# Last norm's row sums moved to TensorE, one tile's scale to GpSimd, spare input loads dropped, last row stores split over two queues, one chunk's weight sums moved

## The reference, cut to what matters

```python
x = layer_norm(ALPHA * x + h, ln1_g, ln1_b)        # ALPHA: 2**0.25, then 4**0.25
# every token goes to its two best of 16, 32 and 32 experts, with weights w1 and w2
f = w1 * expert_a(x) + w2 * expert_b(x)            # expert: (silu(x @ gate) * (x @ up)) @ down
x = layer_norm(ALPHA * x + f, ln2_g, ln2_b)
def layer_norm(u, g, b):
    mu = mean(u); var = mean((u - mu)**2)
    return (u - mu) * rsqrt(var + 1e-5) * g + b
```

## Time and profile before

| | us |
|---|---|
| three runs | 2676.49, 2680.26, 2680.79 (median 2680.26) |
| the profiled execution's own time | 2675.48 |
| its span, first to last instruction | 2673.8 |
| PE busy | 2275.1 (85%) |
| DVE busy | 1024.7 (38%) |
| ACT busy | 561.3 (21%) |
| POOL busy | 290.2 (11%) |
| mean granted TensorE clock, as a share of 2.4 GHz | 0.951 |

### The profile page before, as it was taken

One profiled execution on the slowest core, in us unless ns is written; L12 is line 12 of the kernel. 1 busy time (PEld: TensorE's weight loads), 2 busy tenths in 40 slices (PEclk: granted clock), 3 DMA queues, 4 the chain that ended last, 5 costly groups with the idle time before them and its releaser, 6 DMA issues. The chain is left out here.

```text
span 2673.8 us, 86507 instructions
## 1 busy us (share of the span) xinstructions
PE 2275.1 (85%) x37544; PEld 1611.2 (60%) x37545; DVE 1024.7 (38%) x2635; ACT 561.3 (21%) x1213; POOL 290.2 (11%) x493
## 2 busy tenths in 40 slices
PE   8997988788799888999667789978888988779972
PEld 3445546666588745777545543458887466656751
DVE  1206342222553844333212263046765352223324
ACT  2036211111301721111001131034442111111111
POOL 1001222222100010000000010012333100000001
PEclk9998999999899999999988899989999999999996
DMA  8602169998404008889999942000001289999995
GB/s 341 258 32 95 49 248 368 408 375 321 165 32 160 1 18 323 347 327 428 429 428 428 395 144 102 0 25 3 3 5 65 81 343 427 429 428 428 404 428 218
DMA packets 92529, 635.86 MB, mean 238 GB/s; under 512 B 22869, under 2 KB 43609, under 8 KB 58346
## 3 DMA queue, kind: packets, MB, share of 16 engines
q1 hardware_dynamic: 47984, 584.42, 53.0%
q0 software_dynamic: 13008, 29.41, 3.5%
q10 hardware_dynamic: 31402, 20.06, 2.4%
HBM read 588.69 MB, written 45.12 MB: 237 GB/s over the span
## 5 line engine op out<-in xcount | busy, mean ns | idle before, releaser
L1315 PE MATMUL ps<-ring,arena 128*32 128x128 f32 x13184 | 413.2, 285 | 107.8 <-DMA ring<-in_experts 73.5
L1315 PEld LDWEIGHTS ps<-ring,arena 128*32 128x32 f32 x13184 | 382.2, 115 | 152.7 <-DMA ring<-in_experts 71.9
L1379 ACT ACTIVATE arena<-ps 128x64 f32<-128x64 f32 x292 | 65.5, 224 | 1075.9 <-PE ps L1315 962.0
L1531 DVE TENSOR_TENSOR arena<-arena,ps 128x64 f32<-128x64 f32 x292 | 64.7, 222 | 590.6 <-ACT arena L1379 590.6
L1326 PE MATMUL ps<-ring,arena 128*32 128x256 f32 x3296 | 205.0, 384 | 34.6 <-DVE arena L1534 20.6
L1292 PE MATMUL ps<-x_tok,arena 128*32 128x256 f32 x3456 | 214.9, 388 | 15.8 <-DVE arena L1434 8.2
L1315 PE MATMUL ps<-arena 128*32 128x128 f32 x5504 | 175.1, 287 | 51.3 <-DMA arena<-in_experts 40.0
L1315 PEld LDWEIGHTS ps<-arena 128*32 128x32 f32 x5504 | 161.5, 115 | 70.9 <-DMA arena<-in_experts 45.5
L1265 PE MATMUL ps<-ring,arena 128*128 128x512 f32 x384 | 171.9, 604 | 3.4 <-PEq L2696 1.7
L1326 PEld LDWEIGHTS ps<-ring,arena 128*32 128x32 f32 x3296 | 106.7, 110 | 111.6 <-issue 29.0
L1292 PEld LDWEIGHTS ps<-x_tok,arena 128*32 128x32 f32 x3456 | 119.1, 113 | 74.0 <-issue 24.7
(11 more groups left out here) (476 smaller groups left out, 3106.8 us busy)
## 6 DMA issues: line engine op xcount, KB each, us to landing
ring<-in_experts SPq DMA_DIRECT2D x165, 2048.0 KB, 21.7
arena<-in_experts SPq DMA_DIRECT2D x50, 2048.0 KB, 24.4
xt_mem<-in_experts SPq DMA_DIRECT2D x25, 2048.0 KB
ring<-in_mixer_chunks SPq DMA_DIRECT2D x24, 2048.0 KB, 13.3
xybuf<-arena ACTq DMA_DIRECT2D x608, 32.0 KB, 6.8
xybuf<-arena SPq DMA_DIRECT2D x1, 9216.0 KB, 51.5
xbuf<-arena SPq DMA_DIRECT2D x1, 9216.0 KB, 31.7
arena<-xbuf POOLq DMA_DIRECT2D x176, 32.0 KB, 6.4
```

Of the source, the lines that this page charges most:

```text
L1315: ins = pe.matmul(ps[at, 2 + half, 0:P], xg[:, k, :], w_gu[half][:, k, q, :], start=(k == 0), stop=(k == NK - 1))
L1379: act.activation(silu_g[:, half, :], ps[:, 2 + half, 0:HALF], ACT.Silu).then_inc(s_silu[half], 1)
L1531: dve.tensor_tensor(hidden[:, half, :], silu_g[:, half, :], ps[:, 2 + half, HALF:P], ALU.mult)\
```

## The change

Four edits.

1. `store_quarters` takes the engine. Behind the loop ACT stores quarters 0 and 1 of the last block, SP quarters 2 and 3, in all three layers. SP does so behind all its weight loads.
2. Layer 0: POOL's loop of input loads runs one turn less (8 DMAs of 32 KB less), and its last wait is for 64 counts less of each buffer.
3. `norm_qkv_stage`: `weight_sums(1)` stands behind `update_rows(3)`.
4. `last_norm_stage` is written anew. DVE makes nine diagonal matrices (alpha, and w1 and w2 of each tile on the diagonal) from the identity. PE sums alpha x + w1 y1 + w2 y2 in PSUM with them, six products of 128x512 for each tile, those with alpha of tiles 0 and 1 ahead of the gathers. DVE takes the statistics, ACT normalizes, both from PSUM. POOL does `gain_rows` of tile 0, DVE of tiles 1 to 3, each behind the statistics of the next tile. The second gather of tile 0 has a semaphore of its own.

```diff
--- before.py
+++ after.py
@@ -1148,6 +1148,11 @@
+            def store_quarters(eng, start, b, two):
+                for q in two:
+                    eng.dma_start(xybuf[bass.ds(start, BLK), q * W:(q + 1) * W], y_sb[quarters[q], b, :])\
+                       .then_inc(s_stored[b], 16)
+
             def value(eng, n, low=1, high=MAXB):
...
@@ -1184,6 +1189,9 @@
                             load_chunk(sp, n)
+                    fours = value(sp, slice(E + 2, E + 3), high=MAXB // AHEAD)
+                    sp.wait_ge(s_y, AHEAD * fours + 1)
+                    store_quarters(sp, AHEAD * fours * BLK, AHEAD - 1, (2, 3))
...
@@ -1215,16 +1223,16 @@
                         pool.wait_ge(*at_step("placed", TABLED))
-                        fours = value(pool, slice(E + 2, E + 3), high=MAXB // AHEAD)
+                        fours = value(pool, slice(E + 2, E + 3), 2 * T // BLK // AHEAD, MAXB // AHEAD)
                         pool.wait_ge(*at_step("inputs_sent", 2 * NT * 16))
                         load_inputs(3 * BLK, 0)
-                        with pool.Fori(0, fours) as p:
+                        with pool.Fori(0, fours - 1) as p:
                             for b in range(AHEAD):
...
                         for b in range(AHEAD):
-                            pool.wait_ge(s_loaded[b], fours * 64 + 64)
+                            pool.wait_ge(s_loaded[b], fours * 64)
...
@@ -1357,14 +1365,9 @@
-                    def store_quarters(start, b, two):
-                        for q in two:
-                            act.dma_start(xybuf[bass.ds(start, BLK), q * W:(q + 1) * W], y_sb[quarters[q], b, :])\
-                               .then_inc(s_stored[b], 16)
-
                     act.wait_ge(*at_step("places_ready", 2))
                     for b in range(AHEAD - 1):
-                        store_quarters((SPARE_BLOCK + b) * BLK, b, range(4))
+                        store_quarters(act, (SPARE_BLOCK + b) * BLK, b, range(4))
                     act.wait_ge(*at_step("placed", TABLED))
...
@@ -1374,11 +1377,11 @@
                             for half in range(2):
-                                store_quarters(g * BLK, freed, (2 * half, 2 * half + 1))
+                                store_quarters(act, g * BLK, freed, (2 * half, 2 * half + 1))
                                 act.wait_ge(s_gu[half], g + 1)
...
                     act.wait_ge(s_y, AHEAD * fours + 1)
-                    store_quarters(AHEAD * fours * BLK, AHEAD - 1, range(4))
+                    store_quarters(act, AHEAD * fours * BLK, AHEAD - 1, (0, 1))
                     for b in range(AHEAD):
...
@@ -1555,39 +1558,94 @@
+        second_rows_in = signal("second_rows_of_tile_0_gathered")
+
         def last_norm_stage(alpha, w1, w2, slots_i):
             y1, y2 = view(arena, NK * T, NT, D), view(arena, 2 * NK * T, NT, D)
-            n0, l0, d0, o0 = tail_bases(), loaded.total, dve_b.take(NT), stored.take(16 * NT)
+            diag0, sum0, scaled0 = dve_a.take(2), mm.take(NT), pool_chain.total
+            alpha_diag, *w_diag = (view(slot(0), n * P, P) for n in range(2 * NT + 1))
+            n0, l0, d0, o0 = tail_bases(), loaded.total, dve_b.take(NT - 1), stored.take(16 * NT)
             with nc.Block() as block:
...
                     for j in range(NT):
-                        sp.wait_ge(dve_b.sem, d0 + j + 1)
+                        if j == 0:
+                            sp.wait_ge(pool_chain.sem, scaled0 + 2)
+                        else:
+                            sp.wait_ge(dve_b.sem, d0 + j)
                         sp.dma_start(out[0, j * P:(j + 1) * P, :], x_tok[:, j, :]).then_inc(stored.sem, 16)
...
                 def _(pool):
-                    gather_rows(pool, y1, y2, slots_i)
+                    for j in range(NT):
+                        for n, (y, there) in enumerate(((y1, rows_in[j]), (y2, rows_in[j] if j else second_rows_in))):
+                            pool.indirect_dma_start(out=y[:, j, :], out_offset=None, in_=xybuf,
+                                                    in_offset=bass.IndirectOffsetOnAxis(ap=slots_i[:, n, j:j + 1], axis=0))\
+                                .then_inc(there.sem, 16)
+                    pool.wait_ge(loaded.sem, l0)
+                    pool.wait_ge(ln_done.sem, n0["normed"] + 1)
+                    gain_rows(pool, Chain(pool, pool_chain), 0).then_inc(pool_chain.sem, 1)
+
+                @block.tensor
+                def _(pe):
+                    def add(diag, rows_of, j, **group):
+                        for c in range(2):
+                            ins = pe.matmul(ps[:, 2 * j + c, :], diag, rows_of[:, j, c * CH:(c + 1) * CH], **group)
+                        return ins
+
+                    pe.wait_ge(dve_a.sem, diag0 + 1)
+                    for j in range(2):
+                        add(alpha_diag, x_tok, j, start=True, stop=False)
+                    pe.wait_ge(dve_a.sem, diag0 + 2)
+                    for j in range(NT):
+                        if j >= 2:
+                            add(alpha_diag, x_tok, j, start=True, stop=False)
+                        pe.wait_ge(rows_in[j].sem, n0["rows"][j] + (32 if j else 16))
+                        add(w_diag[j], y1, j, start=False, stop=False)
+                        if j == 0:
+                            pe.wait_ge(second_rows_in.sem, 16)
+                        add(w_diag[NT + j], y2, j, start=False, stop=True).then_inc(mm.sem, 1)
...
                 def _(act):
-                    alpha_rows(act, alpha)
+                    act.preload_act_table(ACT.Sqrt)
                     for j in range(NT):
-                        norm_rows(act, j, n0)
+                        mv = mean_var[:, j, :]
+                        act.wait_ge(stat.sem, n0["stat"] + j + 1)
+                        act.activation(mv[:, 2:3], mv[:, 1:2], ACT.Sqrt, bias=eps_ln).then_inc(sq.sem, 1)
+                        act.wait_ge(scaled.sem, n0["scales"] + j + 1)
+                        act.activation(x_tok[:, j, :], ps[:, 2 * j:2 * j + 2, :].rearrange("p c n -> p (c n)"), ACT.Identity,
+                                       bias=mv[:, 1:2], scale=mv[:, 3:4]).then_inc(ln_done.sem, 1)
...
+                    def statistics(j):
+                        mv = mean_var[:, j, :]
+                        dve.wait_ge(mm.sem, sum0 + j + 1)
+                        for c in range(2):
+                            ins = dve.bn_stats(sums[:, j % 2, 6 * c:6 * c + 6], ps[:, 2 * j + c, :])
+                        link(ins)
+                        dve.bn_aggr(mv[:, 0:2], sums[:, j % 2, :]).then_inc(stat.sem, 1)
+                        dve.wait_ge(sq.sem, n0["sq"] + j + 1)
+                        link(dve.reciprocal(mv[:, 3:4], mv[:, 2:3]))
+                        dve.tensor_scalar(mv[:, 1:2], mv[:, 0:1], mv[:, 3:4], -1.0, ALU.mult, ALU.mult).then_inc(scaled.sem, 1)
+
                     def finish(j):
...
+                    dve.tensor_scalar(alpha_diag, ident, alpha, None, ALU.mult).then_inc(dve_a.sem, 1)
+                    for j in range(NT):
+                        for n, wn in enumerate((w1, w2)):
+                            ins = dve.tensor_scalar(w_diag[n * NT + j], ident, wn[:, j:j + 1], None, ALU.mult)
+                    ins.then_inc(dve_a.sem, 1)
                     dve.wait_ge(loaded.sem, l0)
                     for j in range(NT):
-                        update_rows(dve, link, j, n0, y1, y2, w1, w2)
-                        if j > 0:
+                        statistics(j)
+                        if j > 1:
                             finish(j - 1)
...
@@ -1835,9 +1893,8 @@
                     for j in range(NT):
-                        if j == 3:
-                            weight_sums(1)
                         update_rows(dve, link, j, n0, y1, y2, w1, w2)
+                    weight_sums(1)
                     dve.wait_ge(act_b.sem, n0["taken"] + 2 * NT)
...
```

## The result

The changed kernel takes 2666.49 us (median of 6 runs, 2654.63 to 2671.29) against 2680.18 (6 runs, 2676.49 to 2680.99). The ratio is 0.9947, 95% interval 0.9926 to 0.9968: 13.7 us less, where 14.6 were forecast; the interval is 8.6 to 19.8 us, so that the two lie so close is in part luck. The profiled execution took 2666.24 (span 2664.5, before 2673.8), so it shows only 9.3 of it. Single executions of the changed kernel lie up to 17 apart, and in the ten profiled executions of this document layer 0's last copy of rows, which only the spare loads precede of what the edits touch, starts anywhere from 675.83 to 682.07. So I compare stretches, each from one event of the program to another, and not whole times.

The account below looks back on a forecast made before the run. It took POOL's drain to bound layer 0's end, waits for tile 3 the norm behind, and DVE the last norm. Terms 4.65 + 0 + 0.95 + 4.2 + 4.8 = 14.6 gave 2665.7 us against 2680.3, range 2659 to 2673.

Parts of the forecast that it names:

- Layer 0's end: Barrier behind layer 0: without spare loads POOL's drain ends earlier and split stores bound the stage; 4.65 us won.
- the rival of a 13 us drain: Layer 0's end: POOL's drain lasts 13 as in layers 1 and 2, so only 1.6 us won; chance 0.10.
- Layer 1's end: Split stores behind SP's weight chunks: the chunks' end decides; 0 taken, between 1.1 us lost and 0.95 won.
- Layer 2's end: Split stores with no load left in SP's queue: 0.95 us won, at least 0.5.
- Weight sums: Norm behind layer 0: moved sums let PE turn tile 3 2.95 us earlier without idling; 4.2 won, bounds 2.5 to 4.6.
- The rival of a new wait: Norm behind layer 0: the moved sums end late, PE idles and returns slow; 0.5 us won, not 4.2; chance 0.13.
- Last norm: Last norm: row sums move to PE, the bound moves from DVE to PE; 4.8 us won, bounds 2.0 to 6.
- The diagonals: Last norm, rival: DVE's nine diagonals block POOL's gathers, moving all by 1.8 us, so 3.0 won; chance 0.08.
- PE at half clock: Last norm, rival: twenty products each cost 0.87 us more, 17.4 in all; kernel slower by 2.8; chance 0.02.

Follow-up runs that it names:

- one queue: The changed kernel with all four last stores on ACT's queue again, in all three layers: 2667.57 us (4 runs), ratio 0.995 to the kernel before.
- alpha late: The changed kernel with the last norm's alpha products of tiles 0 and 1 behind the wait for each tile's rows: 2674.84 us (one run).
- spare loads back: The changed kernel with POOL's two spare input loads of layer 0 and their wait put back: 2669.3 us (4 runs), ratio 0.9956 to the kernel before.
- norm back: The changed kernel with the last norm stage of before, where DVE adds and scales all tiles' rows: 2668.9 us (5 runs), ratio 0.9958.

## Why the prediction was right, term by term

The mechanisms held in all five places; one term was mis-sized, and two agreements of numbers are in part luck, as is said at each. Each term by the profiled executions of before and after, with the experiment that isolates it:

- **Layer 0's end, forecast 4.65: 4.68.** The drain starts at 669.5 and takes 3.34 (4 forecast); the rival of a 13 us drain falls. Behind it the stores decide, as forecast, and they came 0.98 sooner. That this is my 0.95 is luck, since I had put all of it down to the issue: from the first store to ACT's last instruction it is 3.32 before, 2.99 with the spare loads and two queues, 3.03 with one queue and no spare loads, 2.34 with both edits. Each edit alone gives 0.3, and the split beside the other 0.7.
- **Layer 1's end, forecast 0: 0.39 lost, of which the split's part is 0.1 at most.** My reason, that the chunks' end decides, holds: the stores' last packet ends 0.28 behind the chunks' last in the changed kernel, 0.32 before. The chunks ended 0.4 later behind the copy of rows, and that lay ahead of the split stores' issue ("one queue" has the numbers); why the copy came sooner against the stream of loads stays open. The rule of the Trainium skill that I had put beside it (DMA: Bandwidth & Descriptors, section Queues, rings and completion order) gave 0.5 lost. The order that it states agrees with the trace, where no packet of SP's pair moves before 1527.14, 2.6 behind its issue; the 0.5 that I had worked out from it doesn't come, since ACT's pair ends only 0.14 ahead of SP's.
- **Layer 2's end, forecast 0.95: 0.66 won.** One queue's 4.05 against 3.39 isolates it. Four issues of 1.75 became two of 0.88, which is 0.87 less; the two queues' transfers then take 0.2 longer to land. The term was too big by these 0.2 and by the 0.08 of issue: its 0.95 is the mis-sized one.
- **Weight sums, forecast 4.2: 3.86.** Tile 3 is turned 35.58 behind the stage's start where it was 38.24: 2.66 sooner, 2.95 forecast. From there to the gapless products it is 8.30 and was 9.50: 1.20, with a wait for the moved sums of 0.28 (0.35 forecast). The 0.3 missing is not of the edit: PE's first sixteen products of the stage took 5.96 at 697.89, where the row of before below has 5.41 ("one queue", with 5.41 too, turns tile 3 at 35.14). The rival of a new wait falls. In the forecast's working tile 3 is ready at 716.5 + 0.7 + 1.24 = 718.4, not 718.6; nothing hangs on it, as PE is busy until 719.2.
- **Last norm, forecast 4.8: 4.79.** PE ends its sums 24.68 behind the start (24.5 forecast) and DVE ends 31.80 behind (31.6 forecast). Tile 0's rows came a microsecond sooner than forecast, which won nothing since PE then waited 1.52 for tile 1's; for the same reason DVE's last pass ends 22.55 behind its first statistics and not the 21.5 forecast. By the prediction's own rows tile 0's second rows would have come at 2634.9 + 1.32 + 5.9 = 2642.1, not 2641.6; PE would still have been at the first two products then, so the sum stands.
- **The diagonals.** Gathers start 1.37, 1.28 and 1.24 apart beside nine diagonals; the first starts 0.68 behind the stage's start in both kernels; the rival's 1.8 is not there, and eight longer copies cost 0.16.
- **PE at half clock.** As a rival that decides the sign it falls: 24 products, of which only the four under the gathers are slow (8 instructions in 5.40). Its mechanism is real in parts: "alpha late" lost 4.3, of which 2.6 by it (an estimate, as above), and one of two profiled executions of the changed kernel lost 3.0 to a longer wait and the slow return behind it.

The row of before that the point on the weight sums names, PE's timeline:

```profile
701.68 5.41 PE L1630 MATMUL ps<-ring,xt_mem 128*128 128x256 f32 x16 [2.56 <-ACT xt_mem L282]
```

Sum of the stretches: 4.68 - 0.39 + 0.66 + 3.86 + 4.79 = 13.6, against 13.7 between the medians and 14.6 forecast. Each stretch is of one execution, and the norm and the last norm scatter by up to 3, so the 0.1 between 13.6 and 13.7 is luck. Of the 1.0 that the sum lies under the forecast, 0.4 is layer 1's, 0.3 layer 2's, and 0.3 the slow products'.

**Why the profiled execution shows 9.3 only.** The missing 4.3 lie in stretches that no edit touches. 0.99 was lost before layer 0's last copy (676.82 against 675.83), and 2.9 between the gapless products and layer 1's end: the lead over before is 7.55 at the gapless products and 4.25 at the stage behind layer 1's end. The last 0.35 is layer 2's. One place in layer 1 where PE stands still can be seen, the same in all kernels. PE's timeline there, before:

```profile
1067.05 0.74 PE L1315 MATMUL ps<-arena 128*32 128x128 f32 x18 [0.77 <-issue]
```

after:

```profile
1061.12 1.28 PE L1323 MATMUL ps<-arena 128*32 128x128 f32 x18 [2.84 <-issue]
```

and with the spare loads back:

```profile
1065.62 0.74 PE L1323 MATMUL ps<-arena 128*32 128x128 f32 x18 [2.84 <-issue]
```

PE stands still ahead of these 18 instructions, for nothing that the profile shows, 0.77 in the first and 2.84 in the others. In ten profiled executions this wait is 0.63 to 3.12. It doesn't explain the lost 2.9. From the gapless products to layer 1's last copy it is 796.57 before and 799.48 after; with the spare loads back, and the same wait of 2.84, it is 796.58, and "alpha late" has a wait of 0.63 and 798.89. Why PE stands still there isn't known either: the DMA share over 1055 to 1063 is 1.02 before and 1.01 after, and the queue that brings instructions has one packet in it in both. Both causes stay open.

## What to carry to other kernels

A stage's end waits for the slowest engine's drain, so look for DMAs that nobody reads: here spare loads on GpSimd's queue cost 3.7 us at the barrier and 0.3 to 0.65 in the stores beside them. The small stores moved to a second queue gained only where that queue was empty and nothing else held the barrier. When sums are moved to TensorE behind an idle stretch, give it real work ahead of the first wait: that work was free here, and 4.3 us of the gain hung on it in the one execution without it.

## What the runs showed of the hardware that I had not expected

- The length of the idle time alone doesn't tell at which clock TensorE comes back. After 3.51 of idle at layer 0's end the 26 products of the next stage took 11.40 in the changed kernel, where after 8.19 they took 14.01. But that isn't the shorter idle's doing: after 3.52 they took 13.09 in five other executions and 14.37 in "norm back", and after 8.21 they took 12.92 with the spare loads back. The next sixteen products follow 2.55 to 2.56 of idle in all ten and take 3.72 to 6.74. PE's timeline in "norm back":

```profile
679.85 14.37 PE L266 MATMUL ps<-cst 128*128 128x512 f32 x26 [3.52 <-PEq L1159]
```

- Indirect DMA issues on GpSimd and DVE copies of 128x512 run side by side nearly undisturbed (0.16 over 2.89 of copies). Of two arithmetic passes on the two engines that meet for about 1, the later one gets 0.9 longer.
- An engine can stand still at the same instruction for 0.6 to 3.1, execution by execution, and the stage around it needn't be longer for it. A difference of 2 us in one profiled execution says nothing until the stretch's own scatter is known.
